# RWKV pipeline: dense and modulation products dealt by the room of each slot instead of evenly

## The reference

```
mod = silu(c) @ w_mod + b_mod            # shift, scale, gate of a layer, from the conditioning alone
h = rmsnorm(x, norm_g) * (1 + scale) + shift
proj = h @ w_in                          # r, k, v, g of RWKV; q, k, v of GLA; qd, kvd of MLA; gates; merge
# RWKV, for each token t, head and direction:
s = s * w_t + (s @ -kk_t) (kk_t * a_t)^T + v_t k_t^T
out_t = s @ r_t
```

## The kernel before

| slot | what TensorE issues, by the names of the code | who must have read out first |
|---|---|---|
| 0 | XS, TB | |
| 1 | TA, X2; of the step before: its part of SO, then U | VectorE (x16) |
| 2 | X4, GT, Ak | ScalarE (X2) |
| 3 | X8, HT; prep: zw, za | ScalarE (X4), VectorE (GT) |
| 4 | T16; of the step before: the rest of SO | ScalarE (X8), VectorE (HT) |
| 5 | Q32, AV | VectorE (T16, XS, Ak) |
| 6 | T32 | ScalarE (Q32) |
| 7 | Q64 | VectorE (T32) |
| 8 | TO, TF | ScalarE (Q64) |
| 9 | Q128 | ScalarE (TO) |
| 10 | TO128 | ScalarE (Q128) |
| 11 | Y | ScalarE (TO128) |
| 12 | TaT | ScalarE (Y) |

## Time and profile before

### The profile page before, as it was taken

One profiled execution on the slowest core, in us unless ns is written; L12 is line 12 of the kernel. 1 busy time (PEld: TensorE's weight loads), 2 busy tenths in 40 slices (PEclk: granted clock), 3 DMA queues, 4 the chain that ended last, 5 costly groups with the idle time before them and its releaser, 6 DMA issues.

```text
span 2998.9 us, 77811 instructions
## 1 busy us (share of the span) xinstructions
PE 2708.9 (90%) x35084; PEld 1643.0 (55%) x35084; DVE 1153.9 (38%) x2873; ACT 1000.0 (33%) x2108; POOL 28.6 (1%) x58
## 2 busy tenths in 40 slices
PE   8988989898987899999999898889998789999997
PEld 2555555555555555555555565556655555555554
DVE  1343444453265443311133445445436544331112
ACT  1333433443254434200014444435325444420000
POOL 0000000000000000000000000000000000000000
PEclk9998999999989899999999999999998889999999
DMA  8101010111110000222231000000010100012221
GB/s 299 44 30 46 31 44 32 45 33 44 52 30 30 20 22 15 86 70 70 78 97 37 24 26 24 18 24 26 17 39 30 30 20 22 15 45 70 71 76 63
DMA packets 35961, 141.95 MB, mean 47 GB/s; under 512 B 4592, under 2 KB 4624, under 8 KB 35248
## 3 DMA queue, kind: packets, MB, share of 16 engines
q1 hardware_dynamic: 31968, 115.82, 12.4%
q0 software_dynamic: 3664, 21.14, 2.0%
HBM read 129.97 MB, written 6.98 MB: 46 GB/s over the span
## 4 chain that ended last, share of the span: by engine, by line
PE 78%; ACT 9%; DVE 9%; issue 3%; DMA 1%; POOL 0%; ACTq 0%; DVEq 0%; SPq 0%
PE psum L552 74%; PE psum L555 4%; DVE tmp L1511 2%; DVE tmp L1503 1%; ACT tmp L1478 1%; DVE tmp L1500 1%; ACT tmp L1202 1%; ACT acts L1202 1%; ACT L1197 1%; DVE tmp L1600 1%; DVE tmp L1507 1%; DMA ring<-units 1%; ACT tmp L1342 0%; ACT L1193 0%; ACT tmp L1193 0%
## 5 line engine op out<-in xcount | busy, mean ns | idle before, releaser
L552 PE MATMUL psum<-hT,ring 128*128 128x128 f32 (+1 forms) x3904 | 1206.1, 453 | 16.7 <-DVE hT L1508 7.6
L552 PEld LDWEIGHTS psum<-hT,ring 128*128 128x128 f32 x3904 | 589.2, 195 | 377.8 <-issue 350.8
L552 PE MATMUL psum<-tmp 64*32 64x32 f32 (+7 forms) x11264 | 599.7, 245 | 66.0 <-DVE tmp L1503 24.3
L552 PEld LDWEIGHTS psum<-tmp 64*32 64x32 f32 (+4 forms) x11264 | 460.1, 134 | 196.7 <-issue 78.0
L1202 ACT ACTIVATE acts<-psum 128x128 f32<-128x128 f32 (+5 forms) x378 | 129.3, 354 | 580.1 <-PE psum L552 578.9
L552 PEld LDWEIGHTS psum<-acts 32*32 32x32 f32 x16320 | 180.5, 106 | 242.6 <-issue 90.5
L552 PE MATMUL psum<-acts 32*32 32x32 f32 x16320 | 222.8, 195 | 64.2 <-ACT acts L1202 24.2
L1202 ACT ACTIVATE tmp<-psum 128x512 f32<-128x512 f32 (+6 forms) x366 | 184.1, 505 | 275.5 <-PE psum L555 226.9
L552 PE MATMUL psum<-acts,ring 128*128 128x512 f32 (+1 forms) x768 | 210.8, 434 | 0.0
L555 PE MATMUL psum<-con_sb,tmp 128*128 128x128 f32 x760 | 130.5, 289 | 76.7 <-DVE tmp L1503 28.9
L1503 DVE TENSOR_TENSOR tmp<-tmp,psum 128x640 f32<-128x640 f32 x32 | 26.3, 821 | 375.4 <-ACT tmp L1490 205.9
(11 more groups left out here) (154 smaller groups left out, 1943.3 us busy)
## 6 DMA issues: line engine op xcount, KB each, us to landing
ring<-units SPq DMA_DIRECT2D x218, 512.0 KB, 3.6
small_sb<-small POOLq DMA_DIRECT2D x2, 3072.0 KB, 11.6
hT<-xT POOLq DMA_DIRECT2D x1, 2560.0 KB, 12.6
tmp<-xT POOLq DMA_DIRECT2D x8, 320.0 KB, 4.7
x_keep<-hT POOLq DMA_DIRECT2D x8, 320.0 KB, 4.9
tmp<-x_keep POOLq DMA_DIRECT2D x8, 320.0 KB, 3.4
yT<-acts POOLq DMA_DIRECT2D x8, 320.0 KB, 3.2
new_rw<-tmp POOLq DMA_DIRECT2D x8, 128.0 KB, 2.0
```

The source lines that it names most:

```text
L552: return nc.tensor.matmul(out, lhsT, rhs, start=start, stop=stop, skip_group_check=True)
```

## The change

`beat_work` alone changes. Before, the 192 quanta of a layer are dealt to the 273 slots evenly, and the 48 modulation products evenly over them. After, all products stand in one list with a cost each; every slot has a cost of its other work from a table (`SLOT_WORK`, for the closing step `LAST_WORK`); a level is sought such that the slots' room up to the level holds all costs, and the list is poured into the rooms in order.

```
+COST_TILE, COST_LAST, COST_MOD, MOD_BEATS = 16, 48, 16, KT
+SLOT_WORK = (36, 52, 36, 22, 28, 22, 11, 5, 6, 6, 6, 16, 6)
+LAST_WORK = (0, 34, 0, 0, 20, 8, 0, 0, 4, 0, 0, 0, 0)
 
 
 def beat_work(l):
 
+    items = [(it, k) for it in DENSE for k in range(KT)]
+    cost = [COST_LAST if k == KT - 1 else COST_TILE for it, k in items]
+    if l + 1 < DEPTH:
+        mods = [(("mod", i // MOD_BEATS), i % MOD_BEATS) for i in range(MOD_BEATS * MOD_GROUPS)]
+        for i, it in reversed(list(enumerate(mods))):
+            at = (2 * i + 1) * len(items) // (2 * len(mods)) if i else 0
+            items.insert(at, it)
+            cost.insert(at, COST_MOD)
+    other = [w for q in range(len(STEPS)) for w in SLOT_WORK] + list(LAST_WORK)
+    low, high = 0.0, float(sum(cost))
+    for _ in range(40):
+        mid = (low + high) / 2
+        room = [max(0.0, mid - w) for w in other]
+        low, high = (low, mid) if sum(room) >= sum(cost) else (mid, high)
+    room = [max(0.0, high - w) for w in other]
     work = [[] for _ in range(BEATS)]
-    tiles = [(it, k) for it in DENSE for k in range(KT)]
-    for q, (it, k) in enumerate(tiles):
-        work[q * BEATS // len(tiles)].append((it, k))
-    if l + 1 < DEPTH:
-        for i in range(MOD_GROUPS * KT):
-            work[(2 * i + 1) * BEATS // (2 * MOD_GROUPS * KT)].append((("mod", i // KT), i % KT))
+    beat, filled_to, done = 0, room[0], 0.0
+    for it, c in zip(items, cost):
+        while beat + 1 < BEATS and done + c / 2 > filled_to:
+            beat += 1
+            filled_to += room[beat]
+        work[beat].append(it)
+        done += c
     return work
```

## The result

| | runs | median us | ratio to before, 95% interval |
|---|---|---|---|
| before | 11 | 2995.8 (2989.98 to 3008.46) | |
| changed | 11 | 3005.4 (2997.58 to 3012.57) | 1.0034 (1.0019 to 1.0049) |

The change made the kernel a third of a per cent slower: 10 us, where 21 us of gain were forecast. The time is inside the wide range that was given (2945 to 3016) and outside the forecast's own (2965 to 2996); the sign is wrong. One execution of a later kernel, 3199.7 us at a mean clock of 0.919, is left out of all figures.

The account below looks back on a forecast made before the run. TensorE was taken as the bound, with 163 us of waits and half clock to win; -24 - 6 - 4 - 3 + 10 + 2 + 7 + 5 - 8 = -21 us took 3000.7 to 2980 us, range 2965 to 2996 (8 in 10: 2945 to 3016).

Parts of the forecast that it names:

- Slots 8 to 12 and the steps with sums: Two gains: fewer uncovered read-out waits in plain steps, 24 us; more cover for reciprocal root and `key_norm` waits, 6 us.
- Slots 3, 5 and 7: Losses: bank under masking, 10 us; SO's bank awaiting VectorE, 2; less cover before T32's read, 7, nearly all layer 1.
- Slots 0 to 2, slot 4, first step: Loss where several slots in a row stand empty: 5 us taken between nothing and 18, 2 of it for first steps.
- that sign of being wrong: The prediction called itself wrong if X2, X4 or T16 wait in most steps.
- Banks of finished items: Gain: fewer tickets landing on the bank of an item just finished, 21 places to 12; 4 us (0 to 7).
- two tiles in a row: Gain: two consecutive tiles take 1.88 us, one alone 1.13; 54 fewer slots hold a product; 3 us, at most 10.
- Clock: Gain: fewer waits near 2 us and above, so a quarter of 34 us at half clock returns: 8 us.
- a sign of being wrong: The prediction called itself wrong if the granted clock moves by more than 0.01.
- no change: Rival: slots 3 to 7 ask back what slots 8 to 12 give, VectorE's 5.1 us being the path; 2999 us, chance 0.20.
- Slower: Rival: TensorE reaches slots 2 and 3 before VectorE is done in every step; +42, 3043 us, chance 0.16.
- Large gain: Rival: added waits in slots 3 to 7 hide behind each other and the clock stays up; -61, 2940 us, chance 0.16.

Follow-up runs that it names:

- the moved product of slot 4: Against one product a slot: in every step layer 0's product of slot 2 and layer 1's of slot 4 go to slot 12; 2951.5 us, 0.9859 of before.
- Layer 0 alone: Changed kernel with layer 1 put back to the old even dealing, only layer 0 dealt by room; 2985.5 us, 0.9963 of before.
- layer 1 alone: Changed kernel with layer 0 put back to the old even dealing, only layer 1 dealt by room; 3008.3 us, 1.0043 of before.
- one product a slot: Changed kernel's cost table replaced by counts: one product in slots 2 and 4 to 11 (layer 0 two in 4 and 6); 2922.0 us, 0.9750 of before.
- the places of the table, in every step: Changed kernel's places dealt by fixed counts, the same in every step, slots 0 to 2 and 4 always empty; 2990.3 us, 0.9982 of before.
- slots 0 to 8 alone: Dealt by counts: one product in each of slots 0 to 8 (layer 0 two in 2 and 4), none in 9 to 12; 3028.0 us, 1.0110 of before.

## Why the prediction was wrong

The forecast was -21 us: -13 of waits and tile lengths, -8 of clock. Measured by the timed executions: +2.7 and +7.7. About half of the miss is the clock, half the waits.

*Slots 8 to 12 and the steps with sums* (-24 and -6): right, -30.0 us. In sum the prices of the earlier trace rows behind an empty slot and the count of empty slots carried over to another order. Of the two waits that were to be nearly gone in layer 0, TO's is (7.8 to 1.4 us in slot 9), Y's is not (8.3 to 7.2 in slot 12): what is left of it are the steps with `key_norm`.

*Slots 3, 5 and 7* (+10, +2, +7): right in size, +11.5, +4.0 and +6.1, slot 3 in part by luck: the masking and the sums that the term priced account for some 8 of it, and the rest are in the main waits of X8 and HT, which the term did not have. Slot 7's loss was to be "nearly all in layer 1": it is, +8.0 there and -1.9 in layer 0.

*Slots 0 to 2, slot 4, first step* (+5, "near the lower end, because X2's row is the usual one"): mis-sized, +11.1. The reason did not hold: one row without a wait behind one empty slot says little of three empty slots in a row. The loss is spread thin: in layer 0, X2, X4, GT and Ak of slots 1 and 2 and T16 of slot 4 wait 1 to 3 us each in 20 steps, much of it put down to "issue"; in layer 1, T16 alone waits 4.3 us, in 8 of 20 steps. None of X2, X4 and T16 waits in most steps, so that sign of being wrong did not come.

*Banks of finished items* (-4) and *two tiles in a row* (-3): of the first nothing is to be seen beside the terms above, so its 4 us belong to the miss; TensorE's time without waits and half clock changed by -2.5 us in the two profiles, so the second fits in size.

*Clock* (-8): this step failed. "Of waits near 2 us and above the terms leave about 11 of 14": so it came, 15 waits of 1.8 us or more before, 12 after. But the half clock follows shorter ones too. Over both pipelines, 13 of before's 14 spells (unbroken stretches) at half clock begin within 3 us of the end of a wait of 1.3 us or more, and 16 of the changed kernel's 17. Such waits number 19 before and 15 after in layer 0, 11 before and 20 after in layer 1, where those of slots 5 and 7 went from 2 to 10: the very waits that the terms of slots 5 and 7 price at a few us. Somewhat under half of all such waits were followed by a spell; layer 1's spells went from 6 to 11, and its granted clock moved by 0.02, where the prediction had set more than 0.01 as a sign of being wrong. So the failed step is the rule that only waits near 2 us and above draw the half clock: a gain of 8 was taken from it, and a loss of 7.7 came. The prediction had such a case as its bound ("a loss of 8 should waits cluster in slots 3 to 5"); the size came, the place was slots 5 and 7 of layer 1.

So, each dealt by room by itself, layer 0 gave 11 us where 16 were forecast, and layer 1 lost 13 us where 5 of gain were. What divides the layers is in part their number of products: after the change layer 0 still has 43 in slots 4 to 6 in 20 steps, layer 1 31 (the prediction's 53 and 39 count a last quantum as three), and in layer 1 slot 7's wait turns on how many lie there, as the moved product of slot 4 showed. The count is not all: in layer 0 slot 7 waits 10.4 us behind the 54 products of before and 8.5 behind 43; that slot 5's waits, 13 to 14 us there, fill the same time is argued and not shown.

Of the rivals, "no change" came nearest: what slots 8 to 12 give is asked back one for one by slots 0 to 7 (-30.0 against +33.1). But VectorE's run of five us, which it named as the path, stands behind slots 5 and 7 alone, 10 of the 33 us. And it lacked the clock. "Slower" asked slots 0 to 5 for 0.9 us a step more than before; they took 27 us in 40 steps, 0.7. "Large gain" had the right size for another dealing: with one product in nearly each slot that a wait follows, half of the waits closed, and with them over half of the time at half clock in the two pipelines' profiles (68 to 27 us).

Open: the parts don't add up exactly. Layer 0 alone changes work and waits by -11.1 and layer 1 alone by +6.4, together -4.7, while the changed kernel has +2.7. And the waits of slots 0 to 4 that are put down to "issue" (12.2 us in layer 0, 8 of them in slots 2 and 3) have no releaser that the profile shows; that slot 3's 4.4 us of them fall to 0.2 with one product in slot 2, and are 4.9 again without it, is all that the runs say.

## What to carry to other kernels

Filler work is worth what the next wait is worth, not what room a slot has: put one piece behind each instruction whose result is read out before the next may start, before any slot gets a second. (That the slots left empty here, 0, 1, 3 and 12, needed none was not tested one by one.) The busy slots of a step were not full of cover; they held the read-outs of masking, of SO and of T32 too. And count the pieces before the wait that comes last of several: with three products there it was 0.19 us a step, with two 0.78.

When a total barely moves, split it by stage first. A gain in one layer and a loss in the other, 11 and 13 us when each was dealt alone, stood behind 10 us here (the sum doesn't close, see above), and the dealing that both led to is 2.5% faster than before and 2.8% faster than the changed kernel.

## What was unexpected of the hardware

Behind a wait of no more than 1.42 us the granted clock fell from 1.00 to 0.53, and the two products that followed took 3.66 us instead of 1.88, so this wait cost more than twice its length; not every such wait did. Over the kernels the cost of the half clock does not follow the sum of the waits: 92.0 us with 62 us of waits in the pipelines (one product a slot), 109.4 with 123 (the places of the table, in every step), 102.9 with 130 (before), 140.0 with 136 (slots 0 to 8 alone). And the clock of one profile can mislead: six profiles with the same dealing in layer 0 show 20 to 44 us at half clock, a spread as wide as the effect that was looked for.
